# Attention over quarters of the heads: the query norm factor moved to where queries leave PSUM, and the next quarter's keys and a head's last score tile moved between transposes and value products

## The reference

```python
cq = rmsnorm_2(u @ w_dq, q_lora_norm)            # 512 x 256, gain per column
q = einsum('bsr,rhd->bshd', cq, w_uq)            # 16 heads x (128 + 64)
q_nope, q_rope = q[..., :128], apply_rope(q[..., 128:], cos, sin)
...
k_nope = einsum('bsr,rhd->bshd', c_kv, w_uk)     # from the shared latent, 128 wide
v      = einsum('bsr,rhd->bshd', c_kv, w_uv)
s = (q_nope @ k_nope + q_rope @ k_rope) * 192 ** -0.5   # causal
o = softmax(s) @ v ;  return o @ w_o
```

## Time and profile before

| | us |
|---|---|
| median of 3 runs (lowest, highest) | 2418.27 (2418.26, 2418.93) |
| the profiled execution, its own time | 2418.04 |
| its span in the trace | 2416.2 |
| PE busy, share of the span | 2342.2 (97%) |
| DVE busy | 1678.2 (69%) |
| ACT busy | 1011.1 (42%) |
| POOL busy | 899.9 (37%) |
| attention, from the first key product of quarter 0 to the first product of `w_o` | 212.5 |

### The profile page before, as it was taken

The page is one execution under the profiler, slowest core; times in us unless marked ns, Lnnn a source line. Parts: engine busy times, 40 slices in busy tenths (PEclk is TensorE's granted clock), DMA queues, the critical chain, the costliest instruction groups (busy, mean ns, idle before and its releaser), DMA issues. The chain is left out here.

```text
span 2416.2 us, 33623 instructions
## 1 busy us (share of the span) xinstructions
PE 2342.2 (97%) x13500; PEld 2023.8 (84%) x13500; DVE 1678.2 (69%) x1629; ACT 1011.1 (42%) x1258; POOL 899.9 (37%) x460
## 2 busy tenths in 40 slices
PE   7999899999989999999999999999989999999998
PEld 6889678778779999989999879999856668799997
DVE  5788578773289687768687669687776743596874
ACT  4324343342254344554354454344433332453443
POOL 1220322211148256348356228256221201383561
PEclk9999999999999999999999999999999999999999
DMA  4221223222323332323342333332310113233322
GB/s 153 72 81 58 70 72 103 87 99 96 100 66 106 109 122 81 93 73 109 110 129 72 97 105 101 110 123 78 91 46 22 35 52 93 86 96 110 123 84 83
DMA packets 217694, 217.11 MB, mean 90 GB/s; under 512 B 10594, under 2 KB 215009, under 8 KB 217569
## 3 DMA queue, kind: packets, MB, share of 16 engines
q1 hardware_dynamic: 217024, 215.14, 28.0%
q10 hardware_dynamic: 544, 0.20, 0.0%
HBM read 213.22 MB, written 2.10 MB: 89 GB/s over the span
## 5 line engine op out<-in xcount | busy, mean ns | idle before, releaser
L1177 PE MATMUL bank<-Xhi,wlo 128*128 128x256 f32 x1152 | 321.3, 279 | 0.0
L1178 PE MATMUL bank<-Xlo,whi 128*128 128x256 f32 x1152 | 321.2, 279 | 0.0
L1179 PE MATMUL bank<-Xhi,whi 128*128 128x256 f32 x1152 | 321.2, 279 | 0.0
L612 POOL TENSOR_TENSOR sums<-raw 128x512 f32<-128x512 f32 x72 | 145.3, 2018 | 428.2 <-DMA raw<-in_ffn_post_wg_dram 160.9
L908 ACT ACTIVATE whi<-raw 128x2048 fp32r<-128x2048 f32 x72 | 138.2, 1920 | 370.3 <-PE bank L1185 227.5
L721 ACT ACTIVATE whi<-raw 128x2048 fp32r<-128x2048 f32 x82 | 156.5, 1908 | 291.6 <-PE bank L1185 276.5
L1183 PE MATMUL bank<-xghi,wlo 128*128 128x512 f32 x624 | 248.7, 399 | 27.1 <-DVE xglo L1778 21.4
L585 POOL TENSOR_TENSOR wlo<-raw,whi 128x2048 fp32r<-128x2048 f32 x24 | 115.7, 4823 | 350.8 <-ACT whi L721 350.8
L1767 DVE TENSOR_TENSOR wlo<-raw,whi 128x2048 fp32r<-128x2048 f32 x58 | 134.0, 2310 | 160.0 <-ACT whi L721 159.9
L1185 PE MATMUL bank<-xghi,whi 128*128 128x512 f32 x624 | 244.7, 392 | 0.0
L1177 PE MATMUL bank<-Xhi,sxlo 128*128 128x256 f32 x864 | 242.0, 280 | 0.2
(11 more groups left out here) (352 smaller groups left out, 6063.5 us busy)
## 6 DMA issues: line engine op xcount, KB each, us to landing
raw<-in_ffn_w_up_dram SPq DMA_DIRECT2D x22, 1024.0 KB, 5.1
raw<-in_ffn_pre_wg_dram SPq DMA_DIRECT2D x22, 1024.0 KB, 5.4
raw<-in_ffn_pre_wu_dram SPq DMA_DIRECT2D x22, 1024.0 KB, 5.4
raw<-in_ffn_post_wg_dram SPq DMA_DIRECT2D x22, 1024.0 KB, 5.4
raw<-in_ffn_post_wu_dram SPq DMA_DIRECT2D x22, 1024.0 KB, 5.4
raw<-in_ffn_pre_wd_dram SPq DMA_DIRECT2D x24, 768.0 KB, 4.4
raw<-in_ffn_post_wd_dram SPq DMA_DIRECT2D x24, 768.0 KB, 4.4
raw<-in_w_in_dram SPq DMA_DIRECT2D x14, 1024.0 KB, 5.0
```

Source lines behind the costliest of these rows:

```text
L612: nc.gpsimd.tensor_tensor(s1, a21, a22, ALU.add).then_inc(adds_done[h], 1)
L1177: nc.tensor.matmul(bank, wl, x, start=first, stop=False, skip_group_check=True)
L1178: nc.tensor.matmul(bank, w, xl, start=False, stop=False, skip_group_check=True)
L1179: return nc.tensor.matmul(bank, w, x, start=False, stop=last, skip_group_check=True)
```

## The change

Eight things change, all in the attention.

1. The factor of the query norm goes into `R` and is multiplied in when DVE takes the query groups out of PSUM (`take` for groups 8 to 11, 14 and 15). The gain alone is put into `cqhi` and `cqlo`. L2368 is gone.
2. The split of quarter 0's weights is cut: key and value columns (0 to 1,023) by ACT, then DVE (semaphore `keys_split`); query columns by ACT, then POOL; of slot 1 only 512 columns (`rope_hi`, `rope_lo`), for quarters 0 to 3.
3. PE makes the keys of quarter 0 straight behind `dq`, and the sums of the squares behind them, in bank 7.
4. The keys of the next quarter are made in the quarter before: heads 0 and 1 behind the transposes of head 2, heads 2 and 3 behind the transposes of head 3 (`next_keys`). DVE copies them out there.
5. The score tile `i` = 3 of heads 1 and 2 is moved behind the transposes of the head before. Its maximum and exponential move with it.
6. The other groups use all eight banks instead of four; value groups banks 4 to 7.
7. The last quarter is written out behind a loop of three passes.
8. SP loads quarter 0's weights ahead of the wait for `down_done`, and pieces of one unit no longer wait for the landing of the pieces before.

```diff
+            def quarter_weights(q):
...
                 sp.wait_ge(wlo_ready[0], split_count(q * 2 + UB["attn"], 0) - 4)
-                base = parts[0]
-                sp.dma_start(r0[:, 0:512], uk[:, bass.ds(q * 512, 512)]).then_inc(part_loaded, 16)
-                sp.dma_start(r0[:, 512:1024], uv[:, bass.ds(q * 512, 512)]).then_inc(part_loaded, 16)
+                if not isinstance(q, int):
+                    sp.wait_ge(keys_split, 1)
...
-                sp.wait_ge(part_loaded, q * 64 + (base + 48))
...
+            quarter_weights(0)
+            sp.wait_ge(down_done, group_no(4, 0, 0))
+            sp.dma_start(rope_q[:, :], A["rope"]).then_inc(rope_q_loaded, 16)
+            with sp.Fori(1, QUARTERS) as q:
+                quarter_weights(q)
...
-            split_lo(UB["dq"] + 3, 1)
-            with pool.Fori(0, QUARTERS) as q:
-                split_lo(q * 2 + (UB["attn"] + 3), 1)
+            pool.wait_ge(whi_ready[0], split_count(UB["attn"], 0))
+            c = slice(1024, UNIT)
+            nc.gpsimd.tensor_tensor(wlo[:, c], raw[:, c], whi[:, c].bitcast(F32), ALU.subtract
+                                    ).then_inc(wlo_ready[0], 4)
+            rope_lo(UB["attn"] + 1)
+            with pool.Fori(0, QUARTERS - 1) as q:
+                rope_lo(q * 2 + (UB["attn"] + 3))
                 split_lo(q * 2 + (UB["attn"] + 2), 0)
+            split_lo(UB["w_o"] + 1, 1)
+            split_lo(UB["w_o"], 0)
...
+            a.wait_ge(groups_done, GB["dq"] + 1)
+            keys_hi(UB["attn"], 0, 0, 1024, 2)
...
-            for u in range(2):
-                split_hi(UB["dq"] + u + 2, u, groups_done, GB["dq"] + (1, 4)[u])
-            for j in range(1, 1 + QR):
-                if j == 1:
-                    root_of(PT[:, 0:T], misc[:, :], QR * P, query_sums, 1)
-                a.wait_ge(latent_ready, j + 1)
-                nc.scalar.activation(tile(cqhi, j - 1), tile(At, j - 1), ACT.Copy).then_inc(latent_hi, 1)
-            with a.Fori(0, QUARTERS) as q:
-                split_hi(q * 2 + (UB["attn"] + 3), 1, groups_done, q * 16 + (GB["attn"] + 10))
-                split_hi(q * 2 + (UB["attn"] + 2), 0, groups_done, q * 16 + (GB["attn"] + 16))
-
-                def exps(h):
-                    for i in range(TC):
+            keys_hi(UB["attn"], 0, 1024, UNIT, 2)
+            query_hi(0)
+            rope_hi(UB["attn"] + 1, 0, GB["dq"] + 4)
+            query_hi(1)
+            root_of(R[:, :], banks[7][:, :], QR * P, query_sums, 1)
...
+                if isinstance(q, int):
+                    split_hi(UB["w_o"] + 1, 1, groups_done, q * 16 + (GB["attn"] + 10))
+                    split_hi(UB["w_o"], 0, groups_done, q * 16 + (GB["attn"] + 16))
+                else:
+                    rope_hi(q * 2 + (UB["attn"] + 3), q + 1, q * 16 + (GB["attn"] + 10))
+                    a.wait_ge(groups_done, q * 16 + (GB["attn"] + 16))
+                    keys_hi(q * 2 + (UB["attn"] + 2), q + 1, 0, UNIT, 4)
...
                     if h < 3:
-                        exps(h + 1)
+                        exps(h + 1, 0, TC - 1 if h < 2 else TC)
...
+                    if h < 2:
+                        exps(h + 1, TC - 1)
...
-            pe.wait_ge(small_step, 3)
-            nc.tensor.matmul(misc[:, :], ones[:, :], PT[:, 0:T], start=True, stop=False)
-            nc.tensor.matmul(misc[:, :], ones[:, :], PT[:, T:2 * T], start=False, stop=True
-                             ).then_inc(query_sums, 1)
             w0 = whi[:, 0:UNIT], wlo[:, 0:UNIT]
             w1 = whi[:, UNIT:2 * UNIT], wlo[:, UNIT:2 * UNIT]
-            with pe.Fori(0, QUARTERS) as q:
-                gb = GB["attn"]
-                unit_ready(q * 2 + UB["attn"], 0)
-                pe.wait_ge(latent_split, 1)
+            gb = GB["attn"]
+
+            def keys(x):
+
+                c = slice(x * P, (x + 1) * P)
+                three(banks[x][:, :], w0[0][:, c], w0[1][:, c], ckhi[:, :], cklo[:, :], True, True
+                      ).then_inc(groups_done, 1)
+
+            pe.wait_ge(keys_split, 1)
+            pe.wait_ge(latent_split, 1)
+            for x in range(4):
+                if x == 1:
+                    pe.wait_ge(evacuated, GB["dq"] + 4)
+                keys(x)
+            pe.wait_ge(small_step, 3)
+            nc.tensor.matmul(banks[7][:, :], ones[:, :], PT[:, 0:T], start=True, stop=False)
+            nc.tensor.matmul(banks[7][:, :], ones[:, :], PT[:, T:2 * T], start=False, stop=True
+                             ).then_inc(query_sums, 1)
+            pe.wait_ge(rstd_log, NORM["mix1"] + 1)
+
+            def attend(q):
+
+                last = isinstance(q, int)
...
                 def group(n):
 
-                    bank_free(q * 16 + (gb + n))
-                    return ring[n % RING][:, :]
+                    pe.wait_ge(evacuated, q * 16 + (gb + n - 7))
+                    return banks[n % 8][:, :]
...
                 for x in range(4):
                     c = slice(x * P, (x + 1) * P)
-                    three(group(x), w0[0][:, c], w0[1][:, c], ckhi[:, :], cklo[:, :], True, True
-                          ).then_inc(groups_done, 1)
-                for x in range(4):
-                    c = slice(x * P, (x + 1) * P)
-                    three(group(4 + x), ckhi[:, c], cklo[:, c], w0[0][:, 512:1024], w0[1][:, 512:1024],
+                    if x == 3:
+                        pe.wait_ge(small_log, 7)
+                        pe.wait_ge(outlo_ready, q * 4 + 1)
+                    three(banks[4 + x][:, :], ckhi[:, c], cklo[:, c], w0[0][:, 512:1024], w0[1][:, 512:1024],
                           True, True).then_inc(groups_done, 1)
+                unit_ready(q * 2 + UB["attn"], 0)
...
-                def scores(h):
+                def scores(h, i0=0, i1=TC):
 
                     if h % 2 == 0:
                         pe.wait_ge(qrope_ready, q * 2 + (h // 2 + 1))
-                    for i in range(TC):
+                    for i in range(i0, i1):
+                        if i == i0:
+                            pe.wait_ge(evacuated, q * 16 + (gb + (11, 12, 15, 16)[h]))
                         if h == 0:
-                            pe.wait_ge(evacuated, q * 16 + (gb + 13 + i))
+                            if i == 3:
+                                pe.wait_ge(evacuated, q * 16 + (gb + 12))
                         else:
                             pe.wait_ge(exp_ready, q * 16 + (4 * (h - 1) + i + 1))
...
+                def next_keys(h):
+
+                    if last:
+                        return
+                    if h == 2:
+                        unit_ready(q * 2 + (UB["attn"] + 2), 0)
+                    for x in (0, 1) if h == 2 else (2, 3):
+                        if h == 2:
+                            pe.wait_ge(exp_ready, q * 16 + (4 * 3 + x + 1))
+                        keys(x)
+
                 scores(0)
                 for h in range(4):
                     if h < 3:
-                        scores(h + 1)
+                        scores(h + 1, 0, TC - 1 if h < 2 else TC)
...
+                    if h < 2:
+                        scores(h + 1, TC - 1)
+                    else:
+                        next_keys(h)
...
+            with pe.Fori(0, QUARTERS - 1) as q:
+                attend(q)
+            attend(QUARTERS - 1)
...
-                hi = ckhi[:, :] if j == 0 else tile(cqhi, j - 1)
-                lo = cklo[:, :] if j == 0 else tile(cqlo, j - 1)
-                src = Ut[:, 0:T] if j == 0 else tile(At, j - 1)
-                nc.vector.tensor_tensor(lo, src, hi.bitcast(F32), ALU.subtract).then_inc(latent_split, 1)
+                if j == 0:
+                    nc.vector.tensor_tensor(cklo[:, :], Ut[:, 0:T], ckhi[:, :].bitcast(F32), ALU.subtract
+                                            ).then_inc(latent_split, 1)
+                else:
+                    nc.vector.scalar_tensor_tensor(tile(cqlo, j - 1), tile(At, j - 1), col("q_lora_norm_2", j - 1),
+                                                   tile(cqhi, j - 1).bitcast(F32), ALU.mult, ALU.subtract
+                                                   ).then_inc(latent_split, 1)
...
                 if u == 0:
                     latent_lo(0)
-            split_lo(UB["dq"] + 2, 0)
-            r = tile(PT, 0)
-            v.wait_ge(small_root, 7)
-            for u in range(2):
-                nc.vector.scalar_tensor_tensor(tile(At, u), tile(At, u), col("q_lora_norm_2", u), r,
-                                               ALU.mult, ALU.mult).then_inc(latent_ready, 1)
-            for j in range(1, 1 + QR):
-                latent_lo(j)
+                    v.wait_ge(whi_ready[0], split_count(UB["attn"], 0) - 2)
+                    nc.vector.tensor_tensor(wlo[:, 0:1024], raw[:, 0:1024], whi[:, 0:1024].bitcast(F32), ALU.subtract
+                                            ).then_inc(keys_split, 1)
+                latent_lo(1 + u)
...
+            for x in range(4):
+                take_keys(0, x)
```

(54 more changed lines are left out.)

33 lines of the change are left out of this document (24 added, 9 removed).

## The result

The changed kernel takes 2398.15 us (median of 4 runs, 2397.8 to 2398.69), the kernel before 2418.27 (2416.77 to 2418.93): ratio 0.9916, 95% interval 0.9904 to 0.9927. The profiled execution took 2398.69 us (span 2396.7).

What follows compares the result with a forecast made beforehand. TensorE, busy for 97% of the span, was taken as the bound. Entry -5.0, quarter starts -2.5, heads -8.5 and switches +0.6 gave -15.4 us from 2418.04, plus 0.2 against the median: 2402.8 us; range 2398.5 to 2409.

Steps and rivals of the forecast that it cites:

- the heads' term: Between transposes and value products: moved score or key tiles cover the 0.60 us wait in 14 of 16 places, -8.5 us.
- The switches: Key tiles behind float32 work begin slower; two more such switches each way in three quarters, +0.6 us.
- Entry: From the last dq product to the first cqhi product: earlier keys and a divided weight split save 5.0 us, bounds -4.1 and -7.9.
- The worked-out 5.8: Entry gain before the clock's price: first cqhi product at 1763.7 instead of 1769.5, 5.8 us.
- half a slow stretch: At the entry, behind about 2.5 us idle: half of the old low-clock loss of 1.7 us, taken as 0.8.
- Starts of the quarters: Narrower rope split and freer banks save 0.7 us in each of quarters 0 to 2, 0.4 in the last: -2.5 us.
- No wait came back: Heads: slack 1.7 us was to keep waits from returning; rival: half comes back, about 2409 us, chance 0.19.
- the slack of 0.4 at head 0: Head 0's transposes follow three tiles, 2.86 us, behind its last tile; first block ready after 2.15 + 0.3.
- whether a running POOL split shuts out the scaling: At head 0, the next weights' split could block the scaling: 0 to 0.2 us a quarter by rule, nothing by rows.
- every case: Whole time: forecast 0.61, entry gives more 0.13, wait comes back half 0.19, no change 0.04, slower 0.03.
- 18 to 19 us less: Rival at the entry: DVE gets in ahead of POOL or no slow stretch comes, 2399.5 us, chance 0.13.
- 5 us more: Rival in the heads: the chain from last score tile to probabilities decides each head, +5, 2425 us, chance 0.03.

Runs made afterwards that it cites:

- keys undone: Changed kernel with the next quarter's four key tiles made together behind head 3's value products again, score tiles still moved: 2402.90 us, ratio to before 0.9936.
- the tiles alone: Kernel before with only the 512-column score tile of heads 1 and 2, its maximum and exponential moved behind the transposes: 2412.12 us, ratio 0.9973.
- the tiles back: Changed kernel with the 512-column score tile of heads 1 and 2, its maximum and exponential put back ahead of the transposes: 2405.68 us, ratio to before 0.9944.
- POOL late at the entry: Changed kernel with POOL's half of the entry's weight split held until DVE made the second latent tile's square: 2395.91 us, ratio to before 0.9907.
- POOL late at both places: Changed kernel with POOL's entry split held until the second square, its first w_o split until the last rope addition: 2396.83 us, ratio to before 0.9909.

## Why the prediction was right in kind and too small

**The step that failed is the heads' term,** "9.7 x 14 / 16 = -8.5 us". It took the idle time in the view of waits (0.60) as the price of a place. The idle time is counted from the modelled end of the transposes, 1.26 us behind their start, while the next product may start 1.10 behind it. What a filled place gives is read from starts: 1.86 us from transposes to value products before, 1.10 until the next product may start after, so 0.76, and some hundredths from the work around them; the runs with tiles or keys undone and the run with the tiles alone all give 0.82. 14 x 0.82 = 11.5, and the places of the last quarter that nothing fills gave some 0.3, of it 0.2 in the waits left there (transposes to value products 1.82 and 1.70 for 1.86 each): 11.8 measured (3 x 3.30 + 1.92).

**The switches, +0.6, did not come on top.** A key place gives 0.82 net of them, as much as a tile place; together with them the heads were forecast at -7.9, measured -11.8: 3.9 of the 5.5 us by which the attention's gain was forecast too small.

**Entry, -5.0 forecast, -6.3 measured.** The mechanism was right in each step, the order of POOL and DVE too; POOL's 3.37 us are a wait of 1.13 until DVE's split ended at 1755.04, and 2.24 of work, forecast 2.3. The worked-out 5.8 stood on an idle time of 2.5 us, which was 2.18; the rest is tenths in tiles and sums. The 0.8 us for half a slow stretch did not arise in either profile of this kernel, and arose in full in the run with the tiles back (1.48; the prediction had 1.7). Half was a mean over two outcomes and no outcome, and that neither profile here had the slow stretch is luck. The Trainium skill (TensorE: Matmul & The Clock Gate, The HAM clock gate) says that the window that decides is free-running, from which the prediction had drawn that the same gap may or may not cost. The traces agree: 2.10 us of idle time came with either clock.

**Starts of the quarters, -2.5 forecast, -2.83 measured:** 3 x 0.82 + 0.37. The rope addition took 0.69 us in quarters 0 to 2 and 2.99 in the last, as forecast.

**No wait came back.** Neither the transposes nor `PT` waited in quarters 0 to 2: the slack of 0.4 at head 0 held. The rule of the Trainium skill (SBUF — State Buffer, section SBUF: two separate sides) that a DVE operation in a two-port mode also takes the pair shared with GpSimd had made the prediction ask whether a running POOL split shuts out the scaling. In the changed kernel this cost nothing, for the split of the next weights ended at 1781.96 and the scaling began at 1781.90. That the scaling is shut out was shown only when POOL was moved: 2.70 for 1.27 us. The forecast had the split over 0.15 us before the scaling; it was still running for 0.06, so head 0 was nearer to that edge than the forecast knew.

**The range** ended at 2398.5 because every case held the heads at 8.5 or less; no case let a measured idle time be worth more than itself. What lies ahead of the attention moved the total the other way: there the profiled execution of the changed kernel lost 1.9 us against that of before, which no term of the forecast held. Three sums of the prediction are a little off and change nothing here: 2418.27 - 15.4 is 2402.9, 18 to 19 us less is about 2399.8, and 5 us more is 2423.3.

## What to carry to other kernels

Price a filled wait by the starts of the instructions around it (start to start before, less the issue time of the work that stays), not by the idle time in the view of waits; here that gave 0.76, with 0.82 measured, for an idle time of 0.60. Before moving a GpSimd operation of some microseconds, list every VectorE operation on wide tiles that works from SBUF to SBUF beneath its whole length, scalings as well as two-input ones: moved off one it may land on the next. When an edit's effect is about a microsecond, judge it by a ledger of starts within the stage. Here the attention repeated to 0.02 us between the two profiles of the changed kernel, where the whole times of one kernel varied by 1 to 3. A clock that falls inside the stage shows in the ledger too, so look at the granted clock beside it.

## What the runs showed of the hardware

The clock behind nearly the same idle time differs between executions. At the key and value projection, in code that no kernel here changes, the first product waits about 3 us; windows of 3.40 us behind it, of before, the changed kernel, the changed kernel once more, and POOL late at the entry (idle times 3.18, 3.20, 3.21, 2.97):

```profile
1396.94:1400.34 3.40, 3.40 (x9) 2.75 (x10) 3.40 (x4) 1.42 (x3) 0.00 (x0) 0.57 0.14 45
```

```profile
1398.66:1402.06 3.40, 3.40 (x10) 2.71 (x11) 3.40 (x4) 1.42 (x3) 0.00 (x0) 0.63 0.15 49
```

```profile
1397.69:1401.09 3.40, 3.40 (x8) 2.72 (x9) 3.40 (x4) 1.42 (x3) 0.00 (x0) 0.50 0.15 49
```

```profile
1397.32:1400.72 3.40, 3.40 (x15) 2.76 (x16) 3.40 (x4) 1.44 (x3) 0.00 (x0) 1.00 0.14 48
```

The last stays at 2.4 GHz, the others fall to 1.2 GHz for most or all of the window. Of all eleven profiles, ten are at 0.50 to 0.63 there. The one at 1.00 has the shortest idle time, but the next shortest, 2.99 us (the score tiles alone), is at 0.56. Early in the span, without any idle time of TensorE, the windows of the changed kernel and of its second profile differ too:

```profile
41.00:44.00 3.00, 3.00 (x9) 2.31 (x8) 2.89 (x3) 0.73 (x1) 0.00 (x0) 0.51 0.00 0
```

```profile
41.00:44.00 3.00, 3.00 (x14) 2.45 (x14) 2.88 (x3) 0.78 (x1) 0.00 (x0) 1.00 0.00 0
```

Between 41 and 44 us some 1.5 of the 1.9 us arise by which the changed kernel's last `dq` product comes later than before's (before has 1.00 in that window). The last `dq` product started anywhere from 1752.50 to 1755.60 us in the eleven profiles. How much of that scatter is clock was not worked out for each profile. What decides the clock in one execution stays open.

Not every VectorE operation is shut out by GpSimd. While POOL's two splits of 9.02 us ran with POOL late at both places, the multiplication of a bank by the factor (0.69), the maxima out of the banks, the reciprocal of 4 columns (0.18) and the scaling of 1 column (0.15) kept their usual times; the scaling of 128 columns from SBUF to SBUF did not (1.71 for 0.28). The wider scalings behind it began when the split was over.
